# A streaming-encoder step on one core: packed query and key norms, a new opening, and the memory keys' norms moved into the output projection

## The reference, cut to what matters

```
z = rmsnorm(x) @ w_in_even                       # one projection: a_b, a_c, a_x, b_q, b_k, b_v, i_q, i_k, i_w
y_a = a_b * conv3(a_c * a_x)                     # mixer A
q = rmsnorm(b_q, per head of 64) * b_q_norm      # mixer B: 8 query heads, 2 key heads
k = rmsnorm(b_k, per head of 64) * b_k_norm
score = sum_h relu(i_q . i_k) * i_w              # indexer
sel = top_k(score)                               # 128 keys for a prompt query, 40 for a sample query
y_b = softmax(q k^T / 8 + bias, over sel) v
x += [y_a, y_b] @ w_out_even
x += cross_attention(rmsnorm(x), mk, mv)         # mk = rmsnorm(rmsnorm(mem) @ w_xk, per head of 256), mv = rmsnorm(mem) @ w_xv
```

## Time and profile before

| | us |
|---|---|
| median of 3 runs | 1684.48 |
| lowest and highest | 1682.56, 1684.67 |
| the profiled execution, its whole time | 1682.37 |
| its span | 1680.6 |
| TensorE matmuls busy | 1595.6 (95%) |
| VectorE busy | 997.4 (59%) |
| ScalarE busy | 636.5 (38%) |
| GpSimd busy | 635.8 (38%) |

### The profile page before, as it was taken

How to read it: one execution, slowest core, us unless ns; L and a number is a source line. 1 busy time by engine, 2 the same in 40 slices (tenths; PEclk the granted TensorE clock), 3 DMA queues, 4 the chain that set the end, 5 groups by cost and what they waited for, 6 DMA issues and landing times.

```text
span 1680.6 us, 31053 instructions
## 1 busy us (share of the span) xinstructions
PE 1595.6 (95%) x11888; PEld 1511.4 (90%) x11890; DVE 997.4 (59%) x1416; ACT 636.5 (38%) x960; POOL 635.8 (38%) x303
## 2 busy tenths in 40 slices
PE   5889987999999999999999979999899999999999
PEld 5789853998699999999999979799699999999999
DVE  5899966456355555455656879556646555045530
ACT  4333356335333333233333665443524333133320
POOL 2235550232043334333434644733124334333332
PEclk9999999999899999999999989999999999999999
DMA  4333330124032222222222322324012223222222
GB/s 170 118 114 112 103 114 1 63 76 163 1 113 81 86 92 100 69 88 87 100 88 91 104 82 84 131 89 175 26 51 77 86 87 103 85 76 87 87 104 89
DMA packets 41714, 153.46 MB, mean 91 GB/s; under 512 B 5344, under 2 KB 5856, under 8 KB 40360
## 3 DMA queue, kind: packets, MB, share of 16 engines
q1 hardware_dynamic: 41640, 152.42, 26.4%
HBM read 145.20 MB, written 9.30 MB: 92 GB/s over the span
## 4 chain that ended last, share of the span: by engine, by line
PE 73%; issue 10%; POOL 6%; DVE 5%; ACT 4%; DMA 0%; POOLq 0%; DVEq 0%; SPq 0%; ACTq 0%
PE PS L831 66%; POOL WLO L411 6%; PE AX L1100 2%; DVE TB L1595 1%; DVE RSTD L1215 1%; ACT WHI L442 1%; PE AX L1010 1%; DVE RB L1597 1%; PE AX L1106 1%; PE AX L1038 1%; PE AX L894 1%; PE PS L1021 1%; ACT LG L626 1%; DVE RB L1599 0%; PE PS L1072 0%
## 5 line engine op out<-in xcount | busy, mean ns | idle before, releaser
L411 POOL TENSOR_TENSOR WLO<-WRAW,WHI 128x1024 fp32r<-128x1024 f32 (+3 forms) x299 | 635.6, 2135 | 1029.5 <-ACT WHI L442 1029.3
L442 ACT ACTIVATE WHI<-WRAW 128x1024 fp32r<-128x1024 f32 (+3 forms) x299 | 268.7, 918 | 690.9 <-PE PS L831 636.5
L831 PE MATMUL PS<-XH,WHI 128*128 128x272 f32 (+1 forms) x2256 | 475.7, 292 | 26.6 <-POOL WLO L411 18.2
L831 PE MATMUL PS<-XH,WLO 128*128 128x272 f32 (+1 forms) x2256 | 469.4, 290 | 0.0
L831 PE MATMUL PS<-XL,WHI 128*128 128x272 f32 (+1 forms) x2256 | 467.1, 289 | 0.0
L831 PEld LDWEIGHTS PS<-XH,WHI 128*128 128x128 f32 x2256 | 360.9, 190 | 34.8 <-POOL WLO L411 17.8
L831 PEld LDWEIGHTS PS<-XL,WHI 128*128 128x128 f32 x2256 | 360.2, 190 | 0.0
L831 PEld LDWEIGHTS PS<-XH,WLO 128*128 128x128 f32 x2256 | 358.4, 190 | 0.0
L831 PE MATMUL PS<-HH,WHI 128*128 128x272 f32 x1216 | 253.0, 289 | 0.7 <-DVE HL L1448 0.7
L831 PE MATMUL PS<-HL,WHI 128*128 128x272 f32 x1216 | 251.8, 288 | 0.0
L831 PE MATMUL PS<-HH,WLO 128*128 128x272 f32 x1216 | 251.8, 288 | 0.0
(11 more groups left out here) (239 smaller groups left out, 1628.1 us busy)
## 6 DMA issues: line engine op xcount, KB each, us to landing
WRAW<-in_w_in_even SPq DMA_DIRECT2D x29, 512.0 KB, 3.5
WRAW<-in_w_up0a SPq DMA_DIRECT2D x22, 512.0 KB, 3.4
WRAW<-in_w_up0b SPq DMA_DIRECT2D x22, 512.0 KB, 3.4
WRAW<-in_w_up1a SPq DMA_DIRECT2D x22, 512.0 KB, 3.4
WRAW<-in_w_up1b SPq DMA_DIRECT2D x22, 512.0 KB, 3.4
WRAW<-in_w_mv SPq DMA_DIRECT2D x16, 512.0 KB, 3.5
WRAW<-in_w_xq SPq DMA_DIRECT2D x16, 512.0 KB, 3.4
WRAW<-in_w_xo SPq DMA_DIRECT2D x16, 512.0 KB, 3.4
```

What stands on the lines that cost most here:

```text
L411: pool.tensor_tensor(WLO[parity][:, first:last], WRAW[parity][:, first:last], WHIf[parity][:, first:last], ALU.subtract).then_inc(lo_done, ...
L442: act.activation(WHI[parity][:, first:last], WRAW[parity][:, first:last], ACT.Copy).then_inc(hi_done, 2 // len(cuts))
L831: ins = pe.matmul(dst, w, x, start=first, stop=last)
```

## The change

1. **Opening.** Only the first 73 parameter columns are loaded first (eps moves to their front), then the first weights, then x. ScalarE begins with a square root of one column (`WARM`) and the high part of chunk 0; it makes all eight XH, then the high part of chunk 1, then the squares. VectorE makes all XL first, then the sums. TensorE runs four matmuls on a zeroed tile before chunk 0. Chunks 0 and 1 are in `IN_HALVES`. Chunk 2 goes to a third PSUM slot (AX banks 2 and 3), and `mean_square(0)` stands inside it.
2. **Packed norms of queries and keys.** The five head turns lose `head_mean`, `head_std`, the reciprocal and the scaling. ScalarE squares each head tile into a buffer of its own. In A tile 0, `query_means` sums all of them with ten matmuls into four groups of 32 PSUM rows; one square root and one reciprocal serve all. In A tiles 1 to 3, `spread_factor` turns 32 packed rows back into a 128-row factor by two matmuls, in the middle of a key chunk, and `query_head` scales the head from PSUM. SP's store of the keys waits for the last of these.
3. **Memory keys' norms** leave the A tiles and `mv0` and are done in `out_even`: `key_square`, `key_sum`, `memory_mean` (before k-step 6 of chunks 1 to 4), `key_std`, `key_head`. The loop of `out_even` is written out.
4. **Top-k rounds.** Three rounds instead of one in each of turns 2 to 4, ahead of the index sum; 8, 10, 10, 9 instead of 9, 12, 12, 10 in the A tiles; six instead of four in `mv0`; one instead of three in the attention.

The core of the diff:

```diff
-IN_HALVES = {*range(C0["in_even"] + EVEN_HEAD, C0["mv0"] + 8), *range(C0["odd"], C0["out_odd"] + 2)}
+IN_HALVES = {C0["in_even"], C0["in_even"] + 1, *range(C0["in_even"] + EVEN_HEAD, C0["mv0"] + 8), *range(C0["odd"], C0["out_odd"] + 2)}
+SPREADS = {(1, 1): 0, (1, 3): 1, (2, 1): 2, (2, 3): 3, (3, 1): 4}
 # SP
-            sp.dma_start(PR[:], a["par"]).then_inc(par_landed, 16)
+            sp.dma_start(PR[:, 0:PAR_FIRST], a["par"][:, 0:PAR_FIRST]).then_inc(par_landed, 16)
+            load(0, a["w_in_even"][0], COLS[0], 0)
...
-            sp.wait_ge(hn_out, HN0["in_even"] + 5)
+            sp.wait_ge(q_out, 5)
 # ScalarE
+            act.activation(WARM[:], par("eps"), ACT.Sqrt)
+            hi(0, 0, COLS[0], 0)
             for m in range(KT):
...
-                norm_tile(0, m, m % 2)
-                if m == 1:
-                    hi(0, 0, COLS[0], 0)
+                act.activation(XH[:, m, :], X[:, m, :], ACT.Copy, scale=par("g_mix", m)).then_inc(xh_ready, 1)
             hi(1, 1, COLS[1], 0)
+            for m in range(KT):
+                if m >= 2:
+                    act.wait_ge(sq_summed, m - 1)
+                act.activation(SQ[:, m % 2, :], X[:, m, :], ACT.Square).then_inc(sq_ready, 1)
+                if m == 2:
+                    ahead(c0)
...
-                head_square(u, QT[:, u, :] if u < 4 else YC[:, 0:T], t0 + 4 + u)
-                head_std(u, False)
 # TensorE
-                if not isinstance(t, int) or t >= 2:
+                if not isinstance(t, int) or t >= 3:
                     pe.wait_ge(evicted, t - 1)
...
+                    dst = AX[:, 2:4, :] if isinstance(t, int) and t == THIRD_SLOT else PS[:, slot, :, :]
+            pe.wait_ge(warm_in, 1)
+            for i in range(4):
+                ins = pe.matmul(AX[:, 0, :], SQA[:, 0:P], SQA[:, 0:512], start=True, stop=True)
+            ins.then_inc(warm_out, 1)
             even_chunk(0)
+            even_chunk(1)
             pe.wait_ge(cst_landed, 32)
-            mean_square(0)
+            even_chunk(2, {1: lambda: mean_square(0)})
...
-                even_chunk(4 + u, lambda: index_group(u))
+                even_chunk(4 + u, {5: lambda: index_group(u)})
...
-                head_mean(u)
+            def query_means():
+                pe.wait_ge(q_sq, 5)
+                pe.wait_ge(cq_landed, 16)
+                pe.wait_ge(relu_done, len(IDX_GROUPS))
+                for i in range(2):
+                    cols = slice(i * H, i * H + H)
+                    for u in range(4):
+                        pe.matmul(AX[32 * u:32 * u + 32, i, 0:H], MEAN_Q, QSQ[:, u, cols], start=True, stop=u > 0)
+                    ins = pe.matmul(AX[0:32, i, 0:H], MEAN_K, SQ[:, 0, cols], start=False, stop=True)
+                ins.then_inc(q_mm, 1)
+
+            def spread_factor(u):
+                if u == 0:
+                    pe.wait_ge(std_read, STD_USES.index(("q", 0)) + 1)
+                    pe.wait_ge(vt_ready, 1)
+                else:
+                    pe.wait_ge(q_out, u)
+                g, pattern, edge = (slice(32 * u, 32 * u + 32), SPREAD, H) if u < 4 else (slice(0, 32), SPREAD_K, HP)
+                for i, cols in enumerate((slice(0, edge), slice(edge, T))):
+                    ins = pe.matmul(AX[:, 2 + i, 0:cols.stop - cols.start], pattern[g, :], IQ[g, 0, cols], start=True, stop=True)
+                ins.then_inc(q_spread, 1)
...
-            linear("out_even", KT, HH, HL, None, 0)
+            def memory_mean(hd):
+                pe.wait_ge(mk_sum, hd + 1)
+                if hd >= 2:
+                    pe.wait_ge(mk_std, hd - 1)
+                pe.matmul(AX[:, hd % 2, 0:MEM], ONES_X, KSA[:, hd % 2, :], start=True, stop=True).then_inc(mk_mm, 1)
+
+            for m in range(LEN["out_even"]):
+                chunk(c0 + m, (c0 + m) % 2, t0 + m, (t0 + m) % 2, KT, HH, HL,
+                      halfway={6: lambda: memory_mean(m - 1)} if 1 <= m <= XHEADS else None)
 # VectorE
+            for m in range(KT):
+                dve.wait_ge(xh_ready, m + 1)
+                dve.scalar_tensor_tensor(XL[:, m, :], X[:, m, :], par("g_mix", m), XHf[:, m, :], ALU.mult,
+                                         ALU.subtract).then_inc(xl_ready, 1)
+            dve.wait_ge(warm_out, 1)
...
+                if u >= 2:
+                    topk(3)
                 index_sum(u)
-                head_rstd(u, T)
...
-                if u >= 2:
-                    topk(1)
+            def query_head(u):
+                dve.wait_ge(q_spread, u + 1)
...
+                dve.scalar_tensor_tensor(halves(QT[:, u, :]), halves(QT[:, u, :]), GQ[:, 0:1], AX[:, 2:4, 0:H], ALU.mult,
+                                         ALU.mult).then_inc(q_out, 1)
...
-            residual("out_even")
+            zero_sum(FEEDS["out_even"])
+            for m in range(LEN["out_even"]):
...
+                norm_tile(FEEDS["out_even"], m, m % 2)
+                if m < XHEADS:
+                    key_sum(m)
+                if 3 <= m < XHEADS + 3:
+                    key_head(m - 3)
```

More of the change, by code:

```diff
@@ L850, in chunk @@
                     cut = [slice(0, first_cut), slice(first_cut, T)] if rh.shape[-1] == T else [slice(0, MEM)]
-                    ins = product([PS[:, slot, i, 0:c_.stop - c_.start] for i, c_ in enumerate(cut)],
+                    dst = AX[:, 2:4, :] if isinstance(t, int) and t == THIRD_SLOT else PS[:, slot, :, :]
+                    ins = product([dst[:, i, 0:c_.stop - c_.start] for i, c_ in enumerate(cut)],
                                   WHI[parity][:, w], WLO[parity][:, w], [rh[:, k, c_] for c_ in cut],
@@ L965, in _ @@
                         even_chunk(EVEN_HEAD + 5 * t + q, behind)
-                    if t and q == 2:
-                        head_mean(HN0["mk0"] + t - 1)
                 if t == 0:
@@ L987, in memory_values @@
                         ins.then_inc(chunk_done, 1)
-                        if l == 0 and ch == 0 and q == 2:
-                            head_mean(HN0["mk0"] + 3)
             memory_values(0)
-            pe.wait_ge(vt_ready, 1)
-            pe.wait_ge(hn_out, 5)
+            pe.wait_ge(q_out, 5)
             pe.wait_ge(evicted, T0["mv0"] + 2)
@@ L1415, in _ @@
                     memory_values(0, 0)
-                    key_head(0, XHEADS - 1)
-                topk((1, 1, 1, 0, 1, 0)[step])
+                topk((2, 1, 1, 0, 1, 1)[step])
             memory_values(0, 1)
@@ L1462, in residual @@
                             norm_tile(norm, m, k)
-            residual("out_even")
+            zero_sum(FEEDS["out_even"])
+            for m in range(LEN["out_even"]):
+                dve.wait_ge(chunk_done, C0["out_even"] + m + 1)
+                dve.tensor_tensor(halves(X[:, m, :]), PS[:, (T0["out_even"] + m) % 2, :, 0:H], halves(X[:, m, :]),
+                                  ALU.add).then_inc(evicted, 1)
+                dve.wait_ge(evicted, T0["out_even"] + m + 1)
+                norm_tile(FEEDS["out_even"], m, m % 2)
+                if m < XHEADS:
+                    key_sum(m)
+                if 3 <= m < XHEADS + 3:
+                    key_head(m - 3)
             def cross(l):
@@ L1753, in _constants @@
     onehot = (bucket[None, :] == np.arange(32)[:, None]).astype(np.float32)
-    return cst, np.concatenate([ident, mask], 1), onehot
+    slot, feature = np.arange(P)[:, None] % 32, np.arange(P)[None, :] // HD
+    spread_q, spread_k = ((slot // 8 == feature + 2 * k).astype(np.float32) / 8 for k in range(2))
+    cq = np.concatenate([spread_q, spread_k, spread_q.T[:, 0:32] / 8, spread_k.T[:, 0:32] / 8], 1)
+    return cst, np.concatenate([ident, mask], 1), onehot, cq
 def kernel(**inputs):
```

229 lines of the change are left out of this document (139 added, 90 removed).

## The result

The changed kernel takes 1673.53 us (median of 4 runs, 1670.82 to 1674.51) against 1684.4 us before: a ratio of 0.9937, 95% interval 0.9922 to 0.9951. It is faster, but by 10.9 us where I had forecast 21, and outside of my range. The profiled execution took 1670.82 us around a span of 1669.0, 11.6 us under the one before.

A forecast was written before the change was run, and what follows sets the result against it. TensorE was taken to bound the kernel, busy nearly throughout, with VectorE busy too from 99 to 206 us. Terms -9.8 - 12.8 - 2.1 + 0 - 0.5 + 5.2 - 0.9 = -20.9 us gave 1663 us; 8-in-10 range 1654 to 1672.

The forecast's parts named there:

- The opening: Start to in_even's chunk 4: first weights earlier, TensorE starts at 8.0 us, chunk 4 at 39.5; -9.8 us.
- my walk: In the opening, chunk 3 starts at 30.5 us, or 32.6 if the last MSQ addition collides with GpSimd's low part.
- The head turns: Five turns, 49.27 to 99.20 us: five waits for squares (8.7) and five head means (4.1) go; -12.8 us.
- rival 2: VectorE stays the bound: turns of 8.0 us, late evictions in the first A tiles; costs 5 to 7 us, 1669 us; 18%.
- The A tiles: 99.20 to 206.64 us: waits and memory head means go (-8.2), query means (2.0) and five spreads (4.1) come; net -2.1 us.
- The store: Store of the keys ahead of the mv0 loads: first mv0 load 5.4 us before the A tiles end; 0 us.
- The output projection: Memory means before k-step 6 of chunks 1 to 4 cost +5.2 us; the earlier table load gives back 0.9.
- So TensorE waits 0.85 and works 0.43, four times: Output projection, chunks 1 to 4: each memory mean waits for VectorE's SQA addition and key_sum; +5.2 us.
- the high end of the term: Output projection: 7 us if VectorE, with key_head's 2.6 us more per tile, falls back over 4 us.
- The table load: Ahead of RSTD: key_std's square root brings its table early, so the 1.28 us load leaves the chain; -0.9 us.
- My tells for being wrong: Waits for CB or UB remain, TensorE stops for a spread, or mv0 weights arrive after the A tiles end.
- the term with the widest ends: The memory means in the output projection: +5.2 us, low end 1.7, high end 7.

The follow-up runs named there:

- sum_first: Changed kernel with VectorE's index sum put back ahead of the three top-k rounds in the turns of chunks 6 to 8; 1674.84 us.
- banks4: Changed kernel with the four memory means in four banks of AX instead of two; 1668.0 us.
- head_first: late_means with the key heads' reciprocals and products ahead of the norm's two operations in four of VectorE's turns; 1663.32 us.
- late_means: Changed kernel with each memory mean at step 1 of the chunk after the next instead of step 6 of the next; 1664.92 us.
- again: The changed kernel run once more, unchanged; 1673.84 us.
- no_key_norm: Changed kernel without the norms of layer 0's memory keys (squares, sums, means, roots, reciprocals, products); 1661.67 us.
- no_warm: Changed kernel with one matmul of 32 columns in place of the four of 512 ahead of chunk 0; 1674.58 us.

## Why the prediction was wrong, point by point

The forecast summed to -20.9 us, the profiles to -11.6. Of the 9.3 us between them 6.4 lie in the output projection and 2.7 in the A tiles; what the other stages were off adds up to 0.2, with misses of up to 1.4 us that cancel.

- **The opening: right, 1 us short.** TensorE's first real matmul came at 9.17, not 8.0, since XL 0 was later; the fast start of chunk 0 came as worked out. Chunk 3 started at 32.85, just past the upper end of my walk; VectorE's eight additions of squares (10.0 us from 14.6 on) and what hangs on them set it. Seven of the eight would do at 0.73 us each, but one took 2.93 beside GpSimd's low part; so mean_square waited 2.4 us, where I had 0.5. No half clock followed the waits of 2.4 and 1.35 us (1.00 in every window from 24 to 40).
- **The head turns: right, 1.4 us more.** Each of five stops was worth 2.84 us. I had 0.82 for the mean itself; by the difference it was 1.1, the rest probably TensorE running dry and filling again at each stop. I didn't test that. My ground for it was only half right: VectorE's turn did shrink as walked, but sum_first shows that a VectorE 2 us later costs TensorE 0.5. What I priced as rival 2 (5 to 7 us for a late VectorE) was far too dear.
- **The A tiles: a size that was off.** CB and UB wait no more, the query means took 1.9 us (2.0 forecast), TensorE waited 0.3 us for the first spread and for no other. These are as forecast. But "a spread is two such matmuls, so one after the other: 0.82, five = 4.1" left out the change of rows: 5 x 1.32 = 6.6, of which 5 x 0.39 is that change and 5 x 0.1 dearer matmuls.
- **The store: in time.** It was issued at 171.94, the first mv0 load at 175.77, 8.7 us ahead of the end of the A tiles (5.4 forecast). mv0 and the start of the attention were 0.6 us longer; TensorE's three waits for WLO inside mv0 grew from 2.7 to 3.9 us in all.
- **The output projection: the step that failed.** "So TensorE waits 0.85 and works 0.43, four times" held for three of the means (0.80 to 0.83; the chunks 1.5 longer and not 1.3), though the two numbers from which the 0.85 came, 5.25 and 4.5 us, give only 0.75. For the fourth I asked only when its input, KSA, is made, and not when its output bank is free. That bank hangs on root 1, that on KST, that on reciprocal 0, and that on a turn of VectorE: a wait of 3.12 us and the half clock behind it, 3.8 us in all by banks4. "With key_head's 2.6 us more per tile VectorE falls back; I find at most 2": it fell back by 4.3 (chunk 7's last matmuls ended at 334.68, its addition began at 338.99), which cost 2.5 us by head_first. Even the high end of the term, 7 us less 0.9, stays under the 10.7 measured. The KSA waits and what came with them cost 4.1 by late_means. 3.8 + 4.1 + 2.5 = 10.4, the difference of again and no_key_norm; another order of the edits could share it out otherwise.
- **The table load**: it left RSTD's chain as forecast.
- What follows RSTD is 0.9 us longer after than before. The runs don't explain it; from RSTD's reciprocal to the end of the span the profiles of all kernels vary between 1323.6 and 1327.0 us, so that 0.9 is within their spread.

My tells for being wrong (CB, UB, a stop for a spread, late mv0 weights) all stayed silent, or nearly so, while I was wrong. None of them looked at the term with the widest ends.

## What to carry to other kernels

For every instruction put into the stream of the bounding engine, trace two chains: when its inputs are made, and when its output buffer is free; a ring of two with a single tile behind it hung on an engine's turn three chunks away. Place such an instruction where both are long past: moving four matmuls by three k-steps bought 7.9 us, and no work was removed (late_means). And before adding a wait to a queue (ScalarE's roots behind `ahead`, SP's load behind the index group), ask what stands behind it.

## What the runs showed of the hardware

- Changing TensorE between matmuls of 128 rows and of 32 and back cost 0.39 us each time, beside the matmuls (three sizes of chunk: 3.74, 4.13, 5.05 us).
- Four fp32 matmuls of 32 rows in a row behind a wait of 0.36 us were followed by 4 us at a granted clock of 0.54 to 0.60; two of them behind the same wait were not. After a wait of 2.4 us in the opening the clock stayed at 1.00, after one of 3.1 us in the projection it was 0.50, and after one of 1.81 us in the kernel before 0.60. The length of a wait alone does not tell.
- At the start of no_warm the 272-column pairs stood 0.45 us apart, as at 274 to 278 us of the kernel after, where the granted clock reads 0.50, the lower of its two levels (1.2 GHz); yet that of 8 to 12 us reads 1.00. The kernel before shows the same at 14 to 18 us. There the duration of the matmuls tells more than that column.
- MAX8 and MATCH_REPLACE8 of 256 columns kept 0.41 to 0.43 us beside GpSimd and without it; an addition of squares (TENSOR_TENSOR, 544 columns) took 2.93 us beside it and 0.73 without, three SCALAR_TENSOR_TENSOR of 384 columns took 3.94 beside it and 1.93 without, and the products of a key head (256 columns, two) 1.95 and 0.88. The Trainium skill ("SBUF — State Buffer", "Who interferes with whom") says that a VectorE instruction with two SBUF inputs contends with a GpSimd instruction that reads SBUF, and one with at most one SBUF input, outside the two-port modes, does not. MAX8, which reads one tile, and the operations that read two agree with it.
